# The MLP's down product in seven half-block products, with relu blocks kept in DRAM

## What is computed

```
h = h + square(relu(rmsnorm(h, g_mlp) @ w1)) @ w2     # w1: 1024 x 4096, w2: 4096 x 1024
return rmsnorm(h, g_final)
```

## Time and profile before

| | us |
|---|---|
| three runs | 3177.0, 3180.99, 3181.78; median 3180.99 |
| profiled execution | 3178.07 |
| its span, first to last instruction | 3176.3 |
| last stage, from 2441.5 (after its first tile) to the last matmul at 3155.7 | 714 |

### The profile page before, as it was taken

One profiled execution on the slowest core, in us unless ns is written; L12 is line 12 of the kernel. 1 busy time (PEld: TensorE's weight loads), 2 busy tenths in 40 slices (PEclk: granted clock), 3 DMA queues, 4 the chain that ended last, 5 costly groups with the idle time before them and its releaser, 6 DMA issues.

```text
span 3176.3 us, 40870 instructions
## 1 busy us (share of the span) xinstructions
PE 3098.6 (98%) x14786; PEld 2524.5 (79%) x14786; DVE 1692.5 (53%) x1937; ACT 1043.0 (33%) x1374; POOL 597.7 (19%) x1031
## 2 busy tenths in 40 slices
PE   8999999999999999997997999999999999999998
PEld 6888888878888888886876888888877888888886
DVE  6545454657767677675336555555545424233343
ACT  4111111344545545453233444444423101111122
POOL 1000000133434444442043222222202000000001
PEclk9999999999999999998998999999999999999998
DMA  3111112121111111115212211111121111111111
GB/s 106 48 47 47 46 46 47 46 93 34 53 33 47 46 33 53 42 31 172 79 47 76 57 34 36 35 35 36 36 73 54 53 47 46 48 46 46 47 47 67
DMA packets 291807, 168.00 MB, mean 53 GB/s; under 512 B 79368, under 2 KB 282120, under 8 KB 291472
## 3 DMA queue, kind: packets, MB, share of 16 engines
q1 hardware_dynamic: 291728, 166.93, 18.3%
HBM read 144.85 MB, written 22.05 MB: 53 GB/s over the span
## 4 chain that ended last, share of the span: by engine, by line
PE 93%; DVE 2%; issue 1%; ACT 1%; POOL 1%; DMA 1%; SPq 0%; DVEq 0%; POOLq 0%; ACTq 0%
PE banks L755 16%; PE banks L757 16%; PE banks L756 16%; PE banks L858 9%; PE banks L859 9%; PE banks L860 9%; PE banks L888 2%; PE banks L1012 1%; PE banks L1094 1%; PE banks L1087 1%; PE banks L901 1%; PE banks L903 1%; PE banks L902 1%; PE banks L880 1%; PE banks L879 1%
## 5 line engine op out<-in xcount | busy, mean ns | idle before, releaser
L858 PE MATMUL banks<-state_a_hi,weights_hi 128*128 128x512 f32 x1352 | 577.9, 427 | 1.1 <-DVE projection_staged L1730 1.1
L859 PE MATMUL banks<-state_a_lo,weights_hi 128*128 128x512 f32 x1352 | 534.4, 395 | 0.0
L860 PE MATMUL banks<-state_a_hi,weights_lo 128*128 128x512 f32 x1352 | 534.2, 395 | 0.0
L755 PE MATMUL banks<-state_a_hi,weights_hi 128*128 128x512 f32 x1176 | 465.9, 396 | 2.3 <-DVE stream_again L1962 1.5
L756 PE MATMUL banks<-state_a_lo,weights_hi 128*128 128x512 f32 x1176 | 465.1, 395 | 0.0
L757 PE MATMUL banks<-state_a_hi,weights_lo 128*128 128x512 f32 x1176 | 465.1, 395 | 0.0
L1226 ACT ACTIVATE weights_hi<-weights_raw 128x1024 fp32r<-128x1024 f32 x226 | 237.7, 1052 | 589.4 <-PE banks L757 507.3
L1587 DVE TENSOR_TENSOR weights_lo<-weights_raw,weights_hi 128x1024 fp32r<-128x1024 f32 x226 | 302.3, 1338 | 155.9 <-ACT weights_hi L1226 154.6
L860 PEld LDWEIGHTS banks<-state_a_hi,weights_lo 128*128 128x128 f32 x1352 | 254.5, 188 | 60.6
L858 PEld LDWEIGHTS banks<-state_a_hi,weights_hi 128*128 128x128 f32 x1352 | 256.2, 190 | 44.0 <-issue 2.6
L859 PEld LDWEIGHTS banks<-state_a_lo,weights_hi 128*128 128x128 f32 x1352 | 256.5, 190 | 39.2 <-issue 2.6
(11 more groups left out here) (309 smaller groups left out, 4802.2 us busy)
## 6 DMA issues: line engine op xcount, KB each, us to landing
weights_raw<-in_mlp_w_dram SPq DMA_DIRECT2D x64, 512.0 KB, 3.7
weights_raw<-in_gdn_w_in_dram SPq DMA_DIRECT2D x33, 512.0 KB, 4.1
weights_raw<-in_pool_w_in_dram SPq DMA_DIRECT2D x32, 512.0 KB, 3.9
weights_raw<-in_sb_w_in_dram SPq DMA_DIRECT2D x32, 512.0 KB, 4.0
weights_raw<-in_pool_w_out_dram SPq DMA_DIRECT2D x16, 512.0 KB, 3.4
weights_raw<-in_sb_w_in_dram SPq DMA_DIRECT2D x32, 256.0 KB, 4.5
mixed_dram<-stick_gate SPq DMA_DIRECT2D x16, 512.0 KB, 3.3
weights_raw<-in_sb_w_out_dram SPq DMA_DIRECT2D x16, 512.0 KB, 4.9
```

Of the source, the lines that this page charges most:

```text
L755: pe.matmul(psum[:, bank, :], whi, hi, start=(k == 0), stop=False)
L858: pe.matmul(psum[:, bank, :], whi, hi, start=(k == 0), stop=False)
L859: pe.matmul(psum[:, bank, :], whi, lo, start=False, stop=False)
L860: last = pe.matmul(psum[:, bank, :], wlo, hi, start=False, stop=(k == end - 1))
```

## The change

**Two phases.** All 32 up tiles come first, in 16 pairs (f, f + 4) of hidden chunks, then the whole down product. DVE forms from the two chunks and the two token halves seven blocks: b11, b21, b22 are relu blocks themselves, t1 to t4 are differences of them. ACT rounds each, DVE writes its rest, and SP stores all seven, 512 KB each with hi and lo, from the one buffer `relu_blocks_staged` to `relu_blocks_dram`, in two DMAs of three and four blocks. DVE writes this buffer again in the next pair after a wait on `relu_stored`. (The block named r12 in the code is not multiplied itself.)

**Seven products for eight.** The down product of a turn g (four again, each with four pairs, 1,024 features) is made for column pairs j (output chunks j and j + 4), each with seven products in the order b11, t2, t3, t1, b21, t4, b22. One product is 4 blocks x 3 = 12 matmuls into one bank: a weight block of 128x512 against a block of 128x512 for each of 4 k. b21, t4 and b22 are accumulated onto a bank after ACT or DVE has taken what stood there. DVE combines the seven into the four quarters of the two chunks (`take_product`): 9 operations of 128x512 for a column pair. The weights of a column pair (two tiles, 1 MB) also give four sums (DVE) and are split block by block, 128x512, six products ahead (`LEAD`; the list `DOWN` sets the order). Column pairs 0 and 1 are interleaved in banks 0 to 3 and 4 to 7, pairs 2 and 3 follow.

**Memory.** The seven blocks of a turn fill the room of states A and B, 2 MB each, all loaded from DRAM. b11 of turn 0 is loaded during the up phase; t2, t3, t1 and b21 lie in B and come after the last up matmul (`up_done`, which DVE gives when it takes the last half), t4 and b22 lie where the staging buffer was and come after the last stores. In turns 1 to 3 each block is loaded once the last column pair has used it.

**Tail.** The chunks become final in the order 0, 4, 1, 5, 2, 6, 7, 3; they are scaled and turned in place in `hacc_o`, and the mean's bank is 1.

The diff, cut to its core (ACT's side, the weight sums and the calls are left out):

```diff
+        relu_stage = nc.alloc_sbuf_tensor_at("relu_blocks_staged", [P, 7, 2, HALF], F32R, offset=a0 + 16 * KB)
...
+        r_dram = nc.dram_tensor("relu_blocks_dram", (7, P, 16, 2, HALF), F32).ap()
...
+        DOWN = [(j, x) for x in PRODUCTS for j in (0, 1)] + [(j, x) for j in (2, 3) for x in PRODUCTS]
...
-            with turns(sp, 4, [(tile, 16)]) as g:
-                for m in range(KC):
-                    load(w_up[:, :, bass.ds(g * D + m * P, P)], KC)
-                for m in range(KC):
-                    load(w_down[:, bass.ds(g * KC, KC), m * P:m * P + P], KC)
+            def load_up(n):
+                f = n // 8 * 8 + n % 8 // 2 + 4 * (n % 2)
+                load(w_up[:, :, f * P:f * P + P], KC)
+            def store_blocks(n):
+                for ready, part in ((2, slice(0, 3)), (4, slice(3, 7))):
+                    sp.wait_ge(relu_lo, 4 * n + ready)
+                    sp.dma_start(r_dram[part, :, n, :, :].rearrange("i p w n -> p i w n"), relu_stage_f[:, part, :, :]).then_inc(relu_stored, 16)
+            def load_down(g, j):
+                for w in range(2):
+                    m = j + 4 * w
+                    sp.dma_start(down_raw[j % 2][w][:, :].rearrange("p (k n) -> p k n", k=KC), w_down[:, g * KC:g * KC + KC, m * P:m * P + P]).then_inc(down_landed[j % 2], 16)
+            def load_block(g, x):
+                sp.dma_start(relu_in_place[x][:, :, :, :], r_dram[BLOCKS.index(x), :, 4 * g:4 * g + 4, :, :]).then_inc(block_landed[x], 16)
+            for n in range(3):
+                load_up(n)
+            for n in range(16):
+                if n < 15:
+                    load_up(2 * n + 3)
+                if n:
+                    store_blocks(n - 1)
+                if n < 14:
+                    load_up(2 * n + 4)
+                if n == 14:
+                    sp.wait_ge(mix_mean, 1)
+                    load_down(0, 0)
+                    sp.wait_ge(relu_stored, 32 * 4)
+                    load_block(0, "b11")
+            sp.wait_ge(weights_lo, tile.value(2))
+            load_down(0, 1)
+            sp.wait_ge(up_done, 1)
+            load_block(0, "t2")
+            load_block(0, "t3")
+            store_blocks(15)
+            load_block(0, "t1")
+            load_block(0, "b21")
+            sp.wait_ge(relu_stored, 32 * 16)
+            load_block(0, "t4")
+            load_block(0, "b22")
+            for g in range(4):
+                for j, last in ((2, 0), (3, 1)):
+                    sp.wait_ge(down_split_lo, N_DOWN * g + DOWN_AT[last, "b22"] + 1)
+                    load_down(g, j)
+                if g < 3:
+                    for j, last in ((0, 2), (1, 3)):
+                        sp.wait_ge(down_split_lo, N_DOWN * g + DOWN_AT[last, "b22"] + 1)
+                        load_down(g + 1, j)
+                    for x in PRODUCTS:
+                        sp.wait_ge(down_done, N_DOWN * g + DOWN_AT[3, x] + 1)
+                        load_block(g + 1, x)
...
+                for q, (j, x) in enumerate(DOWN):
+                    before = PAIR_IN_BANKS[j]
+                    def wait_taken(pair, product):
+                        pe.wait_ge(down_taken, taken.value(TAKEN_AT[pair, product] + 1 - N_TAKEN * (pair == before and j < 2)))
+                    pe.wait_ge(down_split_lo, split.value(q + 1))
+                    if j == 0:
+                        pe.wait_ge(block_landed[x], landed.value(16))
+                    if kind == "first" and j == 0 and x in ("b11", "t2", "t3", "t1"):
+                        pe.wait_ge(bank_free, half.value(1 + (DOWN_BANK[x] - half.fixed) % 4))
+                    elif x in ("b11", "t3", "t1"):
+                        if kind != "first" or j != 1:
+                            wait_taken(before, {"b11": "b21", "t3": "t4", "t1": "b22"}[x])
+                    elif x == "b21":
+                        pe.wait_ge(down_copied, copied.value(j + 1))
+                    elif x in ("t4", "b22"):
+                        pe.wait_ge(down_taken, taken.value(TAKEN_AT[j, {"t4": "t3", "b22": "t1"}[x]] + 1))
+                    bank, onto = down_bank(j, x), x in ("b21", "t4", "b22")
+                    for k in range(4):
+                        whi, wlo = WH[q % 7][:, k * P:k * P + P], WL[q % 7][:, k * P:k * P + P]
+                        hi, lo = relu_blk[x][:, k, 0, :], relu_blk[x][:, k, 1, :]
+                        pe.matmul(psum[:, bank, :], whi, hi, start=(k == 0 and not onto), stop=False, skip_group_check=True)
+                        pe.matmul(psum[:, bank, :], whi, lo, start=False, stop=False, skip_group_check=True)
+                        last = pe.matmul(psum[:, bank, :], wlo, hi, start=False, stop=(k == 3), skip_group_check=True)
+                    last.then_inc(down_done, 1)
...
+            def up_pair(first=False, last=False):
+                for w in range(2):
+                    if not (last and w):
                         split_weights()
-                    if first and m == 0:
+                    if first and w == 0:
                         dve.wait_ge(norm_act, nact.add(2))
-                    if m < KC:
-                        r = y_stage[m % 2]
-                        for h in range(2):
-                            src = take()
-                            hs = slice(h * HALF, h * HALF + HALF)
-                            dve.tensor_tensor(r[:, hs], src, inv[:, hs], ALU.mult).then_inc(bank_free, 1)
-                        dve.wait_ge(bank_free, half.value(4))
-                        dve.scalar_tensor_tensor(out=r[:, :], in0=r[:, :], scalar=0.0, in1=r[:, :], op0=ALU.max, op1=ALU.mult).then_inc(relu_in, 1)
-                        dve.wait_ge(relu_hi, rh.add())
-                        dve.tensor_tensor(A_lo[:, m, :], r[:, :], A_hi[:, m, :].bitcast(F32), ALU.subtract).then_inc(relu_lo, 1)
...
+                    if last and w:
+                        for b in range(5):
+                            down_weights_lo(b)
+                    if not w and not first:
+                        dve.wait_ge(relu_lo, rh.value(-3))
+                    if w and not first:
+                        dve.wait_ge(relu_stored, rst.add(32))
+                    for h in range(2):
+                        src = take()
+                        if last and w and h:
+                            dve.sem_inc(up_done, 1)
+                        hs = slice(h * HALF, h * HALF + HALF)
+                        dve.tensor_tensor(relu_stage_f[:, 1 + h, 1, :] if w else r_first[:, hs], src, inv[:, hs], ALU.mult).then_inc(bank_free, 1)
+                    dve.wait_ge(bank_free, half.value(4))
+                    r = relu_stage_f[:, 1:3, 1, :] if w else r_first[:, :]
+                    dve.scalar_tensor_tensor(out=r, in0=r, scalar=0.0, in1=r, op0=ALU.max, op1=ALU.mult).then_inc(relu_in, 1)
+                rin.add(2)
+                dve.wait_ge(relu_in, rin.value())
+                r11, r12, r21, r22 = r_first[:, 0:HALF], r_first[:, HALF:2 * HALF], relu_stage_f[:, 1, 1, :], relu_stage_f[:, 2, 1, :]
+                t3, t1, t2, t4 = (relu_stage_f[:, 3 + s, 1, :] for s in range(4))
+                dve.tensor_tensor(t1, r12, r11, ALU.subtract).then_inc(relu_sums, 1)
+                dve.tensor_tensor(t3, r22, r12, ALU.subtract).then_inc(relu_sums, 1)
+                dve.wait_ge(relu_sums, rs.value(1))
+                dve.tensor_tensor(t2, r22, t1, ALU.subtract).then_inc(relu_sums, 1)
+                dve.wait_ge(relu_sums, rs.value(3))
+                dve.tensor_tensor(t4, r21, t2, ALU.subtract).then_inc(relu_sums, 1)
+                dve.wait_ge(relu_sums, rs.add(4))
+                dve.wait_ge(relu_hi, rh.add())
+                dve.tensor_tensor(relu_stage[:, 0, 1, :], r11, relu_stage_f[:, 0, 0, :], ALU.subtract).then_inc(relu_lo, 1)
+                for part in (1, 3, 5):
+                    dve.wait_ge(relu_hi, rh.add())
+                    dve.tensor_tensor(relu_stage[:, part:part + 2, 1, :], relu_stage_f[:, part:part + 2, 1, :], relu_stage_f[:, part:part + 2, 0, :], ALU.subtract).then_inc(relu_lo, 1)
...
+                if x == "t2":
+                    dve.wait_ge(down_copied, copied.value(j + 1))
+                    dve.tensor_tensor(u, v, bank, ALU.add).then_inc(down_taken, 1)
+                    dve.wait_ge(down_taken, mine)
+                    for c in (c12, c21):
+                        dve.tensor_tensor(c, c, u, ALU.add).then_inc(down_added, 1)
+                elif x == "t3":
+                    dve.tensor_tensor(v, u, bank, ALU.add).then_inc(down_taken, 1)
+                    dve.wait_ge(down_taken, mine)
+                    dve.tensor_tensor(c22, c22, v, ALU.add).then_inc(down_added, 1)
+                else:
+                    if x == "t1":
+                        dve.wait_ge(down_added, added.value(3 * ADDED_AT[j]))
+                    c = {"t1": c22, "b21": c11, "t4": c21, "b22": c12}[x]
+                    dve.tensor_tensor(c, c, bank, ALU.add).then_inc(down_taken, 1)
```

257 lines of the change are left out of this document (190 added, 67 removed).

## The result

The changed kernel takes 3188.31 us (median of 9 runs, 3186.87 to 3191.72), the kernel before on the same chips 3178.1: ratio **1.0031, interval 1.0021 to 1.0042**. Forecast was 0.3% faster; it is 0.3% slower. A second round gave 3188.58 against 3178.51, 1.0031 again. The profiled execution took 3191.72 us, its span is 3189.8.

What follows compares the result with a forecast made beforehand. TensorE's matmul count was taken as the only bound. -44.8 + 15.5 (up phase) + 18.0 (between phases) + 0.9 (tail) = -10.4 us, giving 3167.7 by the profiled execution, 3170.6 by the median; range 3153 to 3198.

Steps and rivals of the forecast that it cites:

- What bounds the stage: Last stage: TensorE's matmul count is the only bound, 0.2333 us per matmul; every other engine has room.
- The term -44.8: Down product: 1,344 matmuls instead of 1,536, so 192 x 0.2333 = 44.8 us less, if nothing waits.
- The loop through DRAM: Up phase: split, load and stores, landing, VectorE work take 23.6 us per pair against TensorE's 22.4; +15.5 us.
- second rival: Up phase: the next weights load shares engines with the stores, landing 14.8, loop 25.5 us; total 3197; chance 0.18.
- first rival: Up phase: stores land within 11.7 us, so the loop stays under TensorE's pace; total 3155; chance 0.22.
- The third, a slow DMA: Stores and block loads: DMA holds not 410 but, say, 283 GB/s; net +85 us, total 3265; chance 0.06.
- A wait of 1.2 us leaves the clock up: Up phase: TensorE's wait of 1.2 us in each pair was claimed not to lower its clock.
- Between the phases: Up to down product: TensorE waits 5.8 us, then 5.8 for t1, with half clock after; +18.0 us.
- steady down phase: Down product at turn ends: reloaded blocks arrive with 4 us slack or more, so 0; upper end +5.
- The tail: After the last matmul: two chunks become final late and the mean waits for GpSimd's sum; +0.9 us (0.4 to 1.5).
- The last turn: Last turn of the down product: no waiting of TensorE was put into the sum, 0 us.
- fourth rival: Something costed at nothing, a take holding a bank or late GpSimd sum in the last turn: +5 to 20; chance 0.08.

Runs made afterwards that it cites:

- copy first: Changed kernel, last turn only: where VectorE both splits weights and copies a turned chunk, the copy goes ahead of the split; 3185.16 us, ratio 1.0025.

## Why the prediction was wrong

- **What bounds the stage** was right: TensorE, with 0.2333 us a matmul. That this number was a matter of 32 bytes could not be read from the rows of before, since all its products of weight tiles had the same distance. The term -44.8 should have been -48.4, an error in the change's favour.
- **The loop through DRAM** was right in kind: the waits stand before the second tile of a pair, released by the weight split, with VectorE waiting for the stores. The failed step is the landing, 12.9 counted from the split, where 14.2 less 0.3, so 13.9, is measured in the mean. It was taken from one 4,096 KB store; here a load and two stores are issued one behind the other over 1.05 us, and the next load shares the end. The round is 24.7 us in place of 23.6, and the forecast's own form then gives the measured size: 14 x 2.3 - 1.3 = 30.9, against 31.0 measured and 28.1 as the high end. This term decides the sign: with 15.5 in place of 31.0 the change would be some 5 us faster, an estimate from 10.2 - 15.5.
- The **second rival** had the right mechanism for 0.5 to 0.7 of the missing 1.05. It named a loop of 24.35 us as the point from which the sum turns, and the loop was 24.7. The forecast stood 0.75 us from its own tipping point and gave the faster side 0.53, which was too high for a sum that 14 rounds multiply. The first rival needed a landing within 11.7 us, which no round had. The third, a slow DMA, did not come: stores went at 404 GB/s, and the loads between the phases, with the same 64 KB pitch, at 425.
- **"A wait of 1.2 us leaves the clock up"** held for the one wait of that size (1.22 us, ending at 2594.4; clock 1.00 behind it). But the 12 waits were 0.55 to 2.68 us, not 1.2 each, and behind five of the longer ones the clock fell (below). The half-clock stretches, 7.4 us in all, did not add to the total beyond the loop's 31: the period is the loop's and not TensorE's, so they took the place of waiting.
- **Between the phases** 18.0 against 19.5, right in size by errors that cancel: the first gap 5.8 against 6.4, the second 5.8 against 8.7, and the two half-clock stretches 4.4 in sum against 6.4 (2 x 3.2). TensorE reached t1 at T + 26.0, as put (25.8), and started on it at T + 34.5, where 31.6 were put. The steady down phase, 0, was right. The tail, 0.9, measured 1.1 in this profile, but 2.2 in the second one, so that hit is partly luck.
- **The last turn** at nothing was wrong: +5.9, the fourth rival's "late GpSimd sum", though not late but blocking VectorE. It was only a chance of 0.08 where it should have been a term: VectorE's operations with two SBUF operands and the GpSimd adds were both in the code. The Trainium skill had the rule, on the page named above.

In sum: up phase 15.5, last turn 5.9, phases 1.5 and tail 0.2 were put too low, and so was the matmuls' gain, by 3.6: net 19.5. The forecast named 3170.6, 17.7 us under the measured 3188.31. As a difference it missed by 20.6 (-10.4 against +10.2), since the three runs that it started from had a median 2.9 above that of all nine.

## What to carry to other kernels

A store that must land before its staging buffer is used again belongs ahead, in its queue, of any load that waits for later work; one exchange of two lines turned a loss of 10 us into a gain of 22, and with five changes of order into one of 34 (against the kernel before in each case). Where a loop of DMA and VectorE work comes within 5% of TensorE's pace, sum it from the issues it really makes, multiply the error by its rounds, and let that set the chances. Look where weights and moving data lie to each other: 32 bytes of padding gave 51 us to the kernel before, more than all changes of order together gave to the changed one (44); the changed kernel with both is 80 under the kernel before (3097.57 against 3177.91).

## What the runs showed of the hardware

**Matmul pace and placement**, as above: 0.2333, 0.2289 and 0.2267 us for the same matmul at distances of 96, 64 and 0 bytes modulo 128 between its two operands in SBUF.

**The clock can fall after short waits.** Windows of the changed kernel around a wait of 2.68 us (2517.3 to 2520.0):

```profile
2512.00:2517.00 5.00, 5.00 (x23) 3.95 (x21) 4.90 (x8) 4.54 (x5) 0.00 (x0) 1.00 0.00 0
2517.00:2520.00 3.00, 0.34 (x2) 0.00 (x0) 3.00 (x4) 1.06 (x1) 0.00 (x0) 1.00 0.00 0
2520.00:2524.00 4.00, 3.98 (x12) 3.18 (x13) 3.52 (x4) 0.00 (x0) 0.00 (x0) 0.67 0.60 177
2524.00:2528.00 4.00, 4.00 (x17) 3.18 (x17) 0.00 (x0) 0.00 (x0) 0.00 (x0) 0.90 1.03 423
```

The first matmuls behind the wait still step by 0.23 us at 2.4 GHz, and only then does the clock go to 1.2 GHz for some 3 us. The length alone does not decide it. In the second profile of the same kernel, the wait at this place was 2.97 us and the windows behind it show 1.00. The shortest wait behind which the clock fell is 1.76 us (copy first, ending at 2738.2; 0.68 in the 3.8 us behind it), while behind 1.97 us in the changed kernel (ending at 2717.4) it stayed up. In the last stage no fall followed a wait of 1.0 to 1.75 us in any run.

**A GpSimd add stops VectorE** until the add is done where VectorE reads two operands from SBUF (2.90 and 2.06 us in place of 0.69), and not where one operand is in a bank (0.69), as shown in the last turn.
